# Modulation row sums in the MLP of the first block: two float32r products with two columns of ones instead of one float32 product with one column

## What is computed

```python
silu_c = jax.nn.silu(c)
silu_cc = jax.nn.silu(c_ctx)
...
m_lat = (silu_c @ ada_w[i] + ada_b[i]).reshape(B, N_MOD, 1, D)
m_ctx = (silu_cc @ ada_w[i] + ada_b[i]).reshape(N_MOD, D)
```

## Time and profile before

| | us |
|---|---|
| median of 3 runs | 3575.32 |
| lowest and highest | 3569.16, 3576.41 |
| the profiled execution | 3578.14 |
| its span from the first to the last instruction | 3576.3 |
| mean granted clock | 0.981 |
| busy: PE, DVE, ACT, POOL | 3415.3, 1933.9, 1370.4, 535.8 |

### The profile page before, as it was taken

The page is one execution under the profiler, slowest core; times in us unless marked ns, Lnnn a source line. Parts: engine busy times, 40 slices in busy tenths (PEclk is TensorE's granted clock), DMA queues, the critical chain, the costliest instruction groups (busy, mean ns, idle before and its releaser), DMA issues. The chain is left out here.

```text
span 3576.3 us, 47654 instructions
## 1 busy us (share of the span) xinstructions
PE 3415.3 (95%) x18432; PEld 2866.4 (80%) x18432; DVE 1933.9 (54%) x2427; ACT 1370.4 (38%) x2084; POOL 535.8 (15%) x392
## 2 busy tenths in 40 slices
PE   7999999999998999999998998999999999999998
PEld 5776897888777688788876888988888788868887
DVE  4373357777536434777765653533333556554444
ACT  3366244444336624444433443322112243432222
POOL 0031003333103200333321110000000100000000
PEclk9999999999999999999999999999999999999999
DMA  3201224443220122344410002111211021112222
GB/s 130 85 1 59 96 99 159 158 156 120 83 91 1 57 95 103 142 150 150 151 53 18 19 13 83 48 59 59 70 59 59 24 72 59 47 36 95 94 94 71
DMA packets 59481, 287.85 MB, mean 80 GB/s; under 512 B 10816, under 2 KB 12096, under 8 KB 32064
## 3 DMA queue, kind: packets, MB, share of 16 engines
q1 hardware_dynamic: 59328, 285.77, 22.6%
HBM read 283.64 MB, written 2.10 MB: 80 GB/s over the span
## 5 line engine op out<-in xcount | busy, mean ns | idle before, releaser
L169 PE MATMUL ps<-h_hi,w_hi_rest 128*128 128x512 f32 (+1 forms) x1088 | 385.9, 355 | 6.9 <-DVE w_lo_rest L158 4.7
L170 PE MATMUL ps<-h_lo,w_hi_rest 128*128 128x512 f32 (+1 forms) x1088 | 365.4, 348 | 0.0
L1670 POOL TENSOR_TENSOR ada_context<-ada_context,ada_scaled 128x768 f32<-128x768 f32 x112 | 282.8, 2525 | 463.5 <-ACT ada_scaled L1755 458.3
L172 PE MATMUL ps<-h_hi,w_lo_rest 128*128 128x512 f32 (+1 forms) x1088 | 330.9, 348 | 0.0
L158 DVE TENSOR_TENSOR w_lo_mix<-w_raw,w_hi_mix 128x2048 fp32r<-128x2048 f32 x92 | 214.7, 2334 | 183.2 <-ACT w_hi_mix L152 183.1
L169 PE MATMUL ps<-h_hi,w_hi_mix 128*128 128x512 f32 (+1 forms) x736 | 280.8, 382 | 2.2 <-DVE w_lo_mix L158 2.2
L1840 DVE TENSOR_TENSOR y<-ps,y 128x512 f32<-128x512 f32 (+1 forms) x224 | 165.8, 751 | 216.0 <-PE ps L172 215.4
L170 PE MATMUL ps<-h_lo,w_hi_mix 128*128 128x512 f32 (+1 forms) x736 | 279.6, 380 | 0.0
L172 PE MATMUL ps<-h_hi,w_lo_mix 128*128 128x512 f32 (+1 forms) x736 | 279.5, 380 | 0.0
L152 ACT ACTIVATE w_hi_rest<-w_raw 128x2048 fp32r<-128x2048 f32 x80 | 152.6, 1909 | 328.4 <-PE ps L172 316.4
L169 PE MATMUL ps<-hid_hi,w_hi_rest 128*128 128x512 f32 (+1 forms) x768 | 273.2, 356 | 1.9 <-DVE w_lo_rest L158 1.9
(11 more groups left out here) (450 smaller groups left out, 7802.2 us busy)
## 6 DMA issues: line engine op xcount, KB each, us to landing
w_raw<-in_stream SPq DMA_DIRECT2D x205, 1024.0 KB, 4.9
ada_raw<-in_ada_w SPq DMA_DIRECT2D x128, 384.0 KB, 5.1
cmp_w<-in_cmp_w SPq DMA_DIRECT2D x8, 1024.0 KB, 4.9
mla_raw<-in_stream SPq DMA_DIRECT2D x8, 512.0 KB, 3.6
x<-in_x SPq DMA_DIRECT2D x1, 2048.0 KB, 8.7
out<-x SPq DMA_DIRECT2D x8, 256.0 KB, 2.0
x<-in_ctx SPq DMA_DIRECT2D x1, 1024.0 KB, 11.0
consts<-in_consts SPq DMA_DIRECT2D x1, 768.0 KB, 11.7
```

The costliest lines, as they stand in the source:

```text
L169: pe.matmul(out, whi, xhi, start=start, stop=False)
L170: pe.matmul(out, whi, xlo, start=False, stop=False)
L172: last = pe.matmul(out, wlo, xhi, start=False, stop=stop)
L1670: pool.tensor_tensor(ada.context, ada.context, ada.scaled[:, j % 2, :], ALU.add).then_inc(m["context"], 1)
```

## The change

Both rows are split into two parts like the weights. ScalarE copies `ada_latent` and `ada_context` into `ada_sum_hi` in float32r (`sums_hi`, two activations of 128 x 768), VectorE writes the differences into `ada_sum_lo` (`sums_lo`, two subtractions of 128 x 768), and TensorE sums each chunk with two float32r products that accumulate in PSUM, with two columns of ones moving. `ada_sum_hi` lies where `ada_scaled` lies, `ada_sum_lo` where `ada_latent` and `ada_context` lie. A copy of the ones in float32r is written once at the start. The output takes two columns for each sum, of which `take_rows` reads one.

```diff
             def sum_rows(it, quarter):
                 if quarter == 0:
                     pe.wait_ge(m["out"], it)
-                    pe.wait_ge(m["latent"], KT * (it + 1))
-                    pe.wait_ge(m["context"], (KT - 1) * (it + 1))
+                    pe.wait_ge(m["lo"], 2 * (it + 1))
                 for c, v in [(c, v) for c in range(ADA_C) for v in range(2)][3 * quarter:3 * quarter + 3]:
-                    part = (ada.latent, ada.context)[v]
-                    last = pe.matmul(k.ps[:, 3584 + 2 * c + v:3585 + 2 * c + v], part[:, c * P:(c + 1) * P],
-                                     k.c["ones"][:, 0:1], start=True, stop=True)
+                    out = k.ps[:, 3584 + 4 * c + 2 * v:3586 + 4 * c + 2 * v]
+                    pe.matmul(out, ada.hi[:, v, c * P:(c + 1) * P], ada.ones, start=True, stop=False)
+                    last = pe.matmul(out, ada.lo[:, v, c * P:(c + 1) * P], ada.ones, start=False, stop=True)
...
                 if not last_group:
                     split_hi(act, k, n0 + 4, (s["ready"], (T1 + T2) * it + 8), it=it, per=4)
+                if ada and not last_group:
+                    sums_hi(it)
                 if not last_group:
                     split_hi(act, k, n0 + 5, (s["ready"], (T1 + T2) * it + 12), it=it, per=4)
                 if ada and not last_group:
                     take_rows(it)
 
+            def sums_hi(it):
+                act.wait_ge(m["context"], (KT - 1) * (it + 1))
+                act.wait_ge(m["latent"], KT * (it + 1))
+                act.activation(ada.hi[:, 0, :], ada.latent, ACT.Copy).then_inc(m["hi"], 1)
+                act.activation(ada.hi[:, 1, :], ada.context, ACT.Copy).then_inc(m["hi"], 1)
+
             def take_rows(it):
                 act.wait_ge(m["summed"], it + 1)
                 act.activation(k.mod[:, bass.ds((FF_GROUPS * ada.layer + it) * 2 * ADA_C, 2 * ADA_C)],
-                               k.ps[:, 3584:3584 + 2 * ADA_C], ACT.Copy).then_inc(m["out"], 1)
+                               k.ps[:, 3584:3584 + 4 * ADA_C].rearrange("p (c z) -> p c z", z=2)[:, :, 0],
+                               ACT.Copy).then_inc(m["out"], 1)
...
             for t in range(KT):
+                if ada and t == T1:
+                    sums_hi(FF_GROUPS - 1)
                 if ada and t == KT - 1:
                     take_rows(FF_GROUPS - 1)
...
+            def sums_lo(it, v):
+                part = (ada.latent, ada.context)[v]
+                dve.wait_ge(m["hi"], 2 * it + v + 1)
+                dve.tensor_tensor(ada.lo[:, v, :], part, ada.hi[:, v, :].bitcast(F32), ALU.subtract).then_inc(m["lo"], 1)
...
                     if ada and j < KT - T1:
                         latent_rows(it, T1 + j)
+                    elif ada and j in (5, 6):
+                        sums_lo(it, j - 5)
                     if j % 4 == 3 and not last_group:
                         split_lo(dve, k, n0 + 4 + j // 4, it=it, per=4)
...
+            act.activation(k.ones, k.c["ones"][:, 0:2], ACT.Copy)
```

More of the change, by code:

```diff
@@ L1615, in stage_mlp @@
         loaded = [k.sem(f"{name}_ada_loaded{i}") for i in range(KT)]
-        names = ("latent", "scaled", "context", "summed", "out")
+        names = ("latent", "scaled", "context", "hi", "lo", "summed", "out")
         m = {n: k.sem(f"{name}_ada_{n}") for n in names}
@@ L3102, in first_block @@
     ada.scaled = at("ada_scaled", [P, 2, ADA_W], F32, 183)
+    ada.hi, ada.lo = at("ada_sum_hi", [P, 2, ADA_W], F32R, 183), at("ada_sum_lo", [P, 2, ADA_W], F32R, 177)
+    ada.ones = k.ones
     y = at("y1", [P, KT, SEQ], F32, 161)
@@ L3209, in build @@
         k.tiny = at("tiny", [P, 1], F32, 207.75)
+        k.ones = at("ones_r", [P, 2], F32R, 207.78125)
         k.cv, k.mod = at("cvec", [P, KT, 2], F32, 59.25), at("mod", [P, ADA_TURNS * KT * 2], F32, 207)
```

## The result

| | before | changed |
|---|---|---|
| median, us | 3575.86 (4 runs) | 3739.77 (4 runs) |
| lowest and highest | 3569.16, 3578.61 | 3738.18, 3741.07 |
| span of the profiled execution | 3576.3 | 3737.6 |
| mean granted clock | 0.981 | 0.952 |
| one looped group | 46.27 | 58.03 |

The changed kernel is slower by 164 us; the ratio is 1.046, with an interval of 1.0448 to 1.0472. I had forecast 3677 and a range up to 3697. The direction was right, the time lies outside.

What follows compares the result with a forecast made beforehand. TensorE was taken as the bound. Profiled execution 3578.1 + products 0 + waits 76.3 + clock 25.5 = 3679.9; that execution lies 2.8 over the median, so 3677 us was forecast (chance 0.70), range 3647 to 3697.

Steps and rivals of the forecast that it cites:

- What bounds the kernel: TensorE, busy 95% of the span; in the MLP groups each microsecond it works or waits goes to the end.
- The products' cost, 0: Row sums: 24 float32r products replace twelve float32 ones, with the same number and cost of weight loads, 0.11 us apart.
- The 22 us less: Row-sum products: by the rule of four passes for true FP32, their 43.5 us would halve; the forecast did not adopt it.
- the weight loads get shorter: Rival, row sums: float32r loads take 0.06 us as in 64-column rows, 20.5 us less, 3656; chance 0.08.
- The splits on ScalarE and VectorE: Two activations and two subtractions a group add 30 us and 31 us of busy time, without effect of their own.
- The wait: Before the first row-sum product TensorE waits for VectorE's second subtraction: 5.14 us in a looped group, 76.3 us in all.
- The clock: Behind the waits the granted clock falls: 1.7 us for each of fourteen, half for two short ones, sum 25.5.
- The upper bound, 2.6 us: Most that a clock fall behind one wait should cost; 16 x 2.6 = 41.6 us in all.
- a clock that stays high: Rival: the clock keeps its upper level behind the waits, 3677 - 25.5 = 3651; chance 0.09.
- The nearest number, 3720: Rival, row sums: each float32r product runs as two matmuls, 24 more loads a group, 43.5 us on top; chance 0.04.
- the order on each engine: VectorE runs addition 4 to the second subtraction without a gap; ScalarE's activations end about 671.1, before VectorE needs them.

Runs made afterwards that it cites:

- e6: Changed kernel with its float32r row sums moved from tile 11 to row blocks 5 to 8 of the next group's first tile: 3582.30 us, ratio 1.0017.
- e8: Changed kernel, splits and waits kept, with the old twelve float32 one-column products on the unsplit rows: 3740.59 us, ratio 1.0457.
- e1: Changed kernel with its row sums moved from tile 11 into the first four row blocks of the next group's first tile: 3661.44 us, ratio 1.0251.
- e2: e1 plus one line: TensorE still waits for the second subtraction ahead of tile 11. 3677.20 us, ratio 1.0283.
- e7: e6 plus a wait of TensorE for the second subtraction ahead of the next group's first tile: 3625.22 us, ratio 1.0137.
- e4: Changed kernel with 19 float32 matmuls of 128 x 128 on constants ahead of the first quarter's wait: 3678.80 us, ratio 1.0295.
- e10: Built on e6: ones as weights (128 x 16 block), row parts moving, sums gathered in PSUM, six transposes at layer's end: 3554.91 us, ratio 0.994.

## Why the prediction was right and wrong

- **What bounds the kernel** held: a wait of TensorE in these groups went to the end in full, and nothing gave it back.
- **The products' cost, 0.** Right: e6 has a looped group of 46.24 against 46.27, and e8 shows that float32 and float32r give the same time. The 22 us less that the prediction worked out from the four passes on the page FP8 and Floating Point Precision of the Trainium skill (section TensorE Precision Notes) would have shown in e6 and did not. Nor did the weight loads get shorter: 0.11 us from one product to the next.
- **The splits on ScalarE and VectorE, nothing by themselves.** Right: they are all in e6, at 1.0017. ScalarE's busy time grew by 24.8 us and VectorE's by 27.8, where 30 and 31 were forecast.
- **The wait.** Right in place, cause and size: 5.14 forecast for a looped group, 4.95 measured; the idle times alone sum to 72.5 where the term said 76.3. The chain on VectorE came as listed and at the forecast pace. What was shorter is the way from its end to TensorE: 0.06 us (690.28 to 690.34) where one row of the last group had given 0.26.
- **The clock.** This is the step that failed: "I take 1.7 for each of the fourteen waits of over 5 us". The mechanism was there; for a looped group its size was four times as large, 6.8 us, and over the kernel the busy time of TensorE grew by 89.5 us where the term had 25.5. I took the length of the low stretches, 3.4 and 5.1 us, from two places where other work followed the idle time, and carried it to a place where row sums follow. e1 and e2 show that this is what the length hangs on. With dense work behind the same wait (e2) the kernel takes 3677, the time that the sum gave; that it agrees to the microsecond is luck, since the low stretches there run from about 3 to 6 us and not 3.4. The upper bound, 2.6 us, was taken from the same two rows, so the range could not hold the truth either. The kernel before has waits of TensorE in the first group of the same MLP, which the prediction passed over when it said by the third group's row that there is no other wait. They are of the same size, but dense tiles follow, and they too would have given no more than 1.8:

```profile
553.90 0.79 PE L169 MATMUL ps<-hid_hi,w_hi_mix 128*128 128x512 f32 x1 [4.22 <-DVE hid_lo L1827]
...
553.90:557.50 3.60, 3.60 (x9) 2.83 (x10) 3.60 (x2) 1.30 (x2) 3.52 (x2) 0.50 0.00 0
```

  In the trace before, no wait over 0.52 us stands ahead of row sums, so it had no row for this price. The range had to allow for that and did not.
- **Rivals.** None of them had the mechanism: I had a clock that stays high, and none that stays low for longer. The nearest number, 3720, belongs to 48 row-sum matmuls in a group; there are 24 (384 records for sixteen groups). What was said of the order on each engine held.

## To carry to other kernels

A wait of 2 to 6 us put on a busy TensorE costs itself and mostly a stretch at the lower clock behind it, and how long that is depends on the work behind the wait: price it from a place where the same kind of work follows, and put dense work between the wait and small matmuls. Before an operation is made a predecessor of TensorE's next product, look where it stands in its engine's list: behind an addition that waits for TensorE's own last tile it is late by construction, however idle that engine is on average. A sum over partitions with a row's chunks as weights pays a weight load for each; with the ones as weights the same sums cost about half here, 1.4 instead of 2.7 us a group.

## What the runs showed of the hardware that I had not expected

- After 2.07 us of idle time TensorE worked 10.4 to 13.6 us at 1.2 GHz in eight of twelve groups when row sums followed (e1), and about 3.5 us in six of twelve when dense matmuls followed (e7). In the others the clock did not fall. After 4.8 us it fell each time, for 13.2 to 14.4 us (changed kernel) against about 3 to 6 us (e2).
- The clock fell without such a wait, for 6.83 us in the middle of tile 11, in two of twelve groups whose idle time had been filled down to 0.55 us with 128-column float32 matmuls (e4).
- A stationary block of 16 columns with 512 moving columns runs at 0.23 us, the pace of a full block (e10).
